# Column sums of the modulation moved into the next head pair, and an earlier low-rank load and gate tile at the start of the recurrent stage

## The reference, cut to what matters

```python
ada = (c @ w_ada[l] + b_ada[l])[:, None, :]
sh1, sc1, gt1, sh2, sc2, gt2 = jnp.split(ada, 6, axis=-1)
h = rms_norm(x, norm1_w[l]) * (1.0 + sc1) + sh1
...
w_log = -jax.nn.softplus(-(w0 + jnp.tanh(w_low) @ w2).astype(f32)) - 0.5
a = jax.nn.sigmoid((a0 + a_low @ a2).astype(f32))
kk = heads(k * k_k)
kk = kk / jnp.maximum(jnp.sqrt(jnp.sum(kk * kk, axis=-1, keepdims=True)), 1e-12)
...
g_att, g_rwkv = jnp.split(jax.nn.sigmoid(gate_in + b_gate[l]), N_BRANCHES, axis=-1)
```

## Time and profile before

| what | us |
|---|---|
| median of 3 runs | 2282.11 |
| the 3 runs | 2280.17, 2282.11, 2284.14 |
| profiled execution: span from first to last instruction | 2275.2 |
| TensorE busy in it | 2149.8 |
| GpSimd busy | 1039.4 |
| VectorE busy | 1204.5 |
| ScalarE busy | 554.5 |

### The profile page before, as it was taken

The page is one execution under the profiler, slowest core; times in us unless marked ns, Lnnn a source line. Parts: engine busy times, 40 slices in busy tenths (PEclk is TensorE's granted clock), DMA queues, the critical chain, the costliest instruction groups (busy, mean ns, idle before and its releaser), DMA issues.

```text
span 2275.2 us, 39545 instructions
## 1 busy us (share of the span) xinstructions
PE 2149.8 (94%) x16109; PEld 1712.5 (75%) x16109; DVE 1204.5 (53%) x1607; ACT 554.5 (24%) x1206; POOL 1039.4 (46%) x764
## 2 busy tenths in 40 slices
PE   8999999999989989999889999999997899999998
PEld 6888777777767777788857767777676677888886
DVE  7888525466676660301276555665553555656423
ACT  2100012333342121312322222222322213333201
POOL 7777764353443446163343321233101465666663
PEclk9999999999998989999989999999997999999999
DMA  4233222234333322031222211122002332223221
GB/s 134 93 100 104 92 86 82 88 127 143 122 128 114 102 74 93 26 104 47 78 68 59 60 41 51 30 60 59 13 23 85 113 121 80 93 92 101 97 87 66
DMA packets 180343, 189.97 MB, mean 83 GB/s; under 512 B 8142, under 2 KB 161373, under 8 KB 179933
## 3 DMA queue, kind: packets, MB, share of 16 engines
q1 hardware_dynamic: 172288, 181.81, 25.1%
q10 hardware_dynamic: 7900, 5.94, 0.9%
HBM read 179.30 MB, written 8.44 MB: 83 GB/s over the span
## 4 chain that ended last, share of the span: by engine, by line
PE 79%; DVE 14%; ACT 2%; issue 2%; DVEq 2%; DMA 1%; ACTq 0%
PE bank L760 11%; PE bank L762 11%; PE bank L761 11%; PE bank L1293 6%; PE bank L1180 5%; PE bank L1385 3%; PE bank L895 3%; PE bank L897 3%; PE bank L896 3%; PE bank L988 2%; PE bank L790 1%; PE bank L791 1%; PE bank L792 1%; DVE adaacc L2103 1%; PE bank L1196 1%
## 5 line engine op out<-in xcount | busy, mean ns | idle before, releaser
L619 POOL TENSOR_TENSOR wlo<-raws,whi 128x1024 fp32r<-128x1024 f32 (+5 forms) x316 | 684.4, 2166 | 47.3 <-issue 5.1
L617 POOL TENSOR_SCALAR whi<-raws 128x1024 fp32r<-128x1024 f32 (+5 forms) x316 | 334.6, 1059 | 647.6 <-PE bank L1180 270.3
L760 PE MATMUL bank<-hbuf,whi 128*128 128x512 f32 (+2 forms) x840 | 328.5, 391 | 0.0
L762 PE MATMUL bank<-hbuf,wlo 128*128 128x512 f32 (+2 forms) x840 | 327.5, 390 | 0.0
L761 PE MATMUL bank<-hbuf,whi 128*128 128x512 f32 (+2 forms) x776 | 302.3, 390 | 0.0
L593 POOL TENSOR_TENSOR spare<-ones 1x1 f32<-1x1 f32 x100 | 24.1, 241 | 510.6 <-PE bank L762 275.2
L762 PEld LDWEIGHTS bank<-hbuf,wlo 128*128 128x128 f32 (+2 forms) x840 | 156.8, 187 | 34.8
L760 PEld LDWEIGHTS bank<-hbuf,whi 128*128 128x128 f32 (+2 forms) x840 | 156.9, 187 | 34.3 <-POOL wlo L619 0.2
L761 PEld LDWEIGHTS bank<-hbuf,whi 128*128 128x128 f32 (+2 forms) x776 | 144.9, 187 | 31.3
L2247 DVE TENSOR_REDUCE nmax<-bank 128x4 f32<-128x512 f32 (+3 forms) x40 | 21.2, 553 | 214.5 <-PE bank L1119 149.5
L1180 PE MATMUL bank<-hbuf,whi 128*128 128x512 f32 x256 | 101.3, 446 | 0.0
(11 more groups left out here) (475 smaller groups left out, 4715.5 us busy)
## 6 DMA issues: line engine op xcount, KB each, us to landing
adaw<-in_w_ada SPq DMA_DIRECT2D x64, 384.0 KB, 4.5
raws<-in_w_up SPq DMA_DIRECT2D x22, 1024.0 KB, 5.0
raws<-in_w_in SPq DMA_DIRECT2D x41, 512.0 KB, 4.7
raws<-in_w_in SPq DMA_DIRECT2D x18, 1024.0 KB, 5.0
raws<-in_pool_w_in SPq DMA_DIRECT2D x16, 1024.0 KB, 5.4
raws<-in_mla_w_in SPq DMA_DIRECT2D x10, 1024.0 KB, 6.6
raws<-in_pool_w_out SPq DMA_DIRECT2D x8, 1024.0 KB, 5.3
raws<-in_mla_w_out SPq DMA_DIRECT2D x8, 1024.0 KB, 5.6
```

What stands on the lines that cost most here:

```text
L617: G.tensor_scalar(h_, r_, 1.0, 1.0, ALU.mult, ALU.mult)
L619: G.tensor_tensor(l_, r_, f32(h_), ALU.subtract).then_inc(raw_split, 1)
L760: M.matmul(dst, wh, acts[k][0], start=(first and k == 0), stop=False)
L762: mm = M.matmul(dst, wl, acts[k][0], start=False, stop=(last and k == n - 1))
```

## The change

It has two parts. In the latent heads, the column sums of pair i - 1 become `condition_columns(i - 1)`, issued by TensorE inside pair i between slices 6 and 7, into bank 2; ScalarE's copy (`take_condition`) moves behind the fourth exponential of pair i; VectorE's `condition(0)` moves behind `maximum(2)` and `maximum(3)`. The last pair's sums stay where they were. At the recurrent start, the first low-rank load is issued ahead of the combination's copies, gate tile j = 1 of pair 0 is computed ahead of `key_norms(0)`, and the two gate tiles of pair 0 are taken in the order 1, 0.

```diff
--- before.py
+++ after.py
@@ -76,11 +76,14 @@
     if _i == 6:
         HEAD_USES += [("o0", 0, 0), ("o1", 0, 1)]
     if _i == 7:
-        HEAD_USES += [("o0", 1, 0), ("o1", 1, 1), ("o0", 2, 2), ("o1", 2, 3)]
+        HEAD_USES += [("o0", 1, 0), ("o1", 1, 1)]
+    if _i >= 1:
+        HEAD_USES += [("ada", _i - 1, 2)]
+    if _i == 7:
+        HEAD_USES += [("o0", 2, 2), ("o1", 2, 3)]
     if _i + 1 < HEAD_PAIRS:
         HEAD_USES += [(name, _i + 1, b) for name, b in PROJ_BANKS]
-    HEAD_USES += [("ada", _i, 0)]
-HEAD_USES += [("o0", 3, 0), ("o1", 3, 1)]
+HEAD_USES += [("ada", HEAD_PAIRS - 1, 0), ("o0", 3, 0), ("o1", 3, 1)]
 FILLS = {"pool": (12,) * 4, "pool_out": (2,) * 4, "lat": (2, 1, 2, 1), "mz": (1,) * 4,
          "heads": tuple(sum(use[2] == b for use in HEAD_USES) for b in range(4)),
          "mla_out": (2,) * 4, "att": (9,) * 4, "lora": (1, 0, 1, 1), "rkv": (8, 8, 8, 0), "mix": (4,) * 4,
@@ -207,6 +210,7 @@
 MADE_ALL = [sum(2 * (len(level) > w) for level in LEVELS) for w in range(2)]
 HEAD_ROWS = (slice(0, CH), slice(CH, P))
 GATE_BANK = (0, 6)
+GATE_ORDER = ((1, 0), (0, 1))
 LEVEL_BANK = ((1, 6), (7, 3))
 
 
@@ -399,6 +403,11 @@
             return evac[b], fill(ph, b) + t // 4 + 1
 
 
+        def lora_loads(p):
+
+            return ((lw2[0:64, :], a["w2_2"][0, :, p * P:(p + 1) * P]),
+                    (lw2[64:128, :], a["a2_2"][0, :, p * P:(p + 1) * P]))
+
         def gate_rows(p):
 
             return xT[:, p % 2 * 2 * S:(p % 2 * 2 + 2) * S]
@@ -1025,7 +1034,10 @@
                 scores(1)
                 turned(0)
                 turned(1)
-                project(i, 5, 9)
+                project(i, 5, 7)
+                if i >= 1:
+                    condition_columns(i - 1)
+                project(i, 7, 9)
                 values(0)
                 values(1)
                 scores(2)
@@ -1049,6 +1061,9 @@
                 values(6)
                 values(7)
                 project(i, 29, 37)
+
+            def condition_columns(i):
+
                 pe.wait_ge(sem("ada.acc"), (i + 1) * DT)
                 cols_bank = take_bank("ada", i)
                 for t in range(6):
@@ -1060,6 +1075,7 @@
             pe.wait_ge(sem("krope"), 1)
             for i in range(HEAD_PAIRS):
                 attention(i)
+            condition_columns(HEAD_PAIRS - 1)
             for n in range(16):
                 out_slice(3, n)
             pe.wait_ge(sem("m.lo"), 16)
@@ -1172,9 +1188,10 @@
             def gate_part(p, n):
 
                 part, i = divmod(n, 3)
-                j, k = divmod(part, DT)
+                turn, k = divmod(part, DT)
+                j = GATE_ORDER[min(p, 1)][turn]
                 s, odd, dst = STRIP0["rkv"] + p * 3 + 2, p % 2, bank[GATE_BANK[j]]
-                if i == 0 and j == 0 and k in (0, first_half(DT)):
+                if i == 0 and turn == 0 and k in (0, first_half(DT)):
                     strip_ready(s, int(k > 0))
                 wh, wl = [w[odd][:, k * 256 + j * P:k * 256 + (j + 1) * P] for w in (whi, wlo)]
                 mm = M.matmul(dst[:, :], wl if i == 2 else wh, h_out[k][int(i == 1)],
@@ -1412,9 +1429,11 @@
 
             pe.wait_ge(sem("cmb.used"), 4)
             lora_products(0)
+            for n in range(3 * DT):
+                gate_part(0, n)
             key_norms(0)
             pe.wait_ge(evac[0], fill("rkv", 0) + 1)
-            for n in range(6 * DT):
+            for n in range(3 * DT, 6 * DT):
                 gate_part(0, n)
             wide_part(1)
             for p in range(PAIRS):
@@ -1569,6 +1588,11 @@
                     b = HEAD_USE[name, i][0]
                     A.copy(vN[:, n * 512:(n + 1) * 512], bank[b][:, :]).then_inc(evac[b], 1)
 
+            def take_condition(i):
+                b = HEAD_USE["ada", i][0]
+                act.wait_ge(sem("ada.col"), i + 1)
+                A.copy(ada[:, i * 6:(i + 1) * 6], bank[b][:, 0:6]).then_inc(evac[b], 1)
+
             def upper_part(t):
                 act.wait_ge(sem("m.y"), t // 2 * 4 + 4)
                 A.copy(y2H[:, t * S:(t + 1) * S], tile(zm, t)).then_inc(sem("m.hi"), 1)
@@ -1609,6 +1633,8 @@
                 exponentials(3)
                 if late:
                     upper_part(late)
+                if i >= 1:
+                    take_condition(i - 1)
                 take_both(1)
                 exponentials(4)
                 exponentials(5)
@@ -1640,9 +1666,6 @@
                         A.activation(z, z, ACT.Silu).then_inc(sem("m.silu"), 1)
                 if i < 7:
                     take_values(i + 1)
-                act.wait_ge(sem("ada.col"), i + 1)
-                A.copy(ada[:, i * 6:(i + 1) * 6], bank[HEAD_USE["ada", i][0]][:, 0:6])\
-                    .then_inc(evac[HEAD_USE["ada", i][0]], 1)
 
             act.wait_ge(sem("norm.lo"), NORM0["n_kv"]["lo"] + 2)
             score_bank, turn_bank = (bank[4], bank[5]), bank[6]
@@ -1651,6 +1674,7 @@
             take_values(0)
             for i in range(HEAD_PAIRS):
                 attention(i)
+            take_condition(HEAD_PAIRS - 1)
             upper_part(14)
             upper_part(15)
 
@@ -1727,6 +1751,8 @@
                           scratch[2].rearrange(nat, p=P, h=ATT_HEADS)).then_inc(sem("st.f0"), 16)
             act.wait_ge(sem("st.f0"), 16)
             act.wait_ge(sem("att.pv"), units_before)
+            for dst, src in lora_loads(0):
+                act.dma_start(dst, src).then_inc(sem("lw.ld"), 16)
             for pr in range(4):
                 if pr >= 1:
                     act.wait_ge(sem("cmb.pe"), pr)
@@ -1744,8 +1770,7 @@
             A.activation(glow[0:32, S:2 * S], glow[0:32, S:2 * S], ACT.Sigmoid).then_inc(sem("lora.act"), 1)
 
             def load_lora(p):
-                for dst, src in ((lw2[0:64, :], a["w2_2"][0, :, ds(p * P, P)]),
-                                 (lw2[64:128, :], a["a2_2"][0, :, ds(p * P, P)])):
+                for dst, src in lora_loads(p):
                     act.dma_start(dst, src).then_inc(sem("lw.ld"), 16)
 
             def load_gate(p):
@@ -1847,7 +1872,6 @@
                 A.activation(aT[p % 2][:, :], bank[3][:, :], ACT.Copy, scale=SCAN_SCALE ** -2).then_inc(sem("gn.y"), 1)
 
             act.wait_ge(sem("att.at"), 4)
-            load_lora(0)
             key_squares(0)
             sigmoids(0)
             load_lora(1)
@@ -2142,9 +2166,9 @@
                 if i == 6:
                     lower_part(6)
                     lower_part(7)
-                condition(0)
                 maximum(2)
                 maximum(3)
+                condition(0)
                 divide(2)
                 divide(3)
                 condition(1)
@@ -2387,13 +2411,13 @@
 
             def take_gates(q):
 
-                for j in range(2):
-                    if j == 0:
+                for turn, j in enumerate(GATE_ORDER[min(q, 1)]):
+                    if turn == 0:
                         if q < 2:
                             dve.wait_ge(sem("x_kept"), 16)
                         else:
                             dve.wait_ge(sem("gt.kept"), (q - 1) * 16)
-                    product_ready(STRIP0["rkv"] + q * 3 + 2, j)
+                    product_ready(STRIP0["rkv"] + q * 3 + 2, turn)
                     V.tensor_copy(tile(xT, q % 2 * 2 + j), bank[GATE_BANK[j]][:, :]).then_inc(sem("gt.taken"), 1)
 
             def centred(p):
```

## The result

| | median us (runs) | profiled execution: time, span |
|---|---|---|
| before | 2281.14 (6; 2278.66 to 2284.14) | span 2275.2 |
| after | 2266.36 (6; 2265.15 to 2273.91) | 2266.18, span 2264.4 |

The ratio is 0.9931, interval 0.991 to 0.9952: 14.8 us or 0.65% less, where 2266.0 was forecast. The two profiled spans differ by 10.8 us only.

What follows compares the result with a forecast made beforehand. TensorE, busy 2149.8 of 2275.2 us, was taken as the bound. Terms 6.5 + 3.2 + 6.2 + 1.5 - 1.0 = 16.4 us less gave a span of about 2258.8; with 6.9 to the median, 2266 us, range 2260 to 2273.

Steps and rivals of the forecast that it cites:

- ends of pairs 0 to 4: Latent heads: TensorE's 1.31 us wait for VectorE before the column sums goes at five pair ends, 6.5 us less.
- pair 5: End of pair 5: moving the sums saves 5.4 to 7.0 us, VectorE being late with low parts; 6.2 taken.
- pair 6: End of pair 6: VectorE late again, so 1.5 us less; 4.4 with the slow clock counted.
- clock behind pairs 0 and 1: Stretch from `scores(0)` to `scores(1)`: both clock falls gone, 2 x (6.2 - 4.6) = 3.2 us less.
- recurrent start: Start of the recurrent stage: 0.3 of the 9.9 us weight wait gained, charges against it; counted 1.0 us slower.
- The wait of `scores(1)`: Behind pair 5: a new TensorE wait of 3.9 us that may lower the clock once more, costing 1.6.
- the four waits forecast: Recurrent start: waits of about 3, 2, 4 and 4 us before low-rank products, both key sums and bonus sums.
- The charge for GpSimd: Recurrent start: GpSimd's earlier strips delay VectorE, between 0 and two or three delays of 1.4 us; 0.5 taken.
- The charge of 1.0: Whole recurrent part counted as 1.0 us slower, with 0.3 faster and 4 slower as ends.

Runs made afterwards that it cites:

- e9_twice: The changed kernel with the column sums of pairs 0 to 6 issued twice over, same result; 2281.64 us, 0.9999 of before.
- e4_warm: The kernel before with 6 extra 512-column products (30 in pair 5) filling TensorE's wait at pair ends; 2268.84 us, 0.9954 of before.
- e6_gated: The changed kernel with low parts of the output from pairs 5 and 6 shifted later, behind divisions of pairs 6 and 7; 2255.52 us, 0.9882 of before.
- f1_after: The changed kernel, both parts, timed once more on the second chip; 2265.17 us, 0.9925 of before.
- e2_rec: The kernel before with part 2 alone: early first low-rank load and new gate tile order; 2287.94 us, 1.0033 of before.
- e3_load: The kernel before with the early low-rank load alone, gate tiles kept in place; 2293.26 us, 1.0066 of before.

## Why the prediction was right

The time was forecast within 0.4 us, which is closer than the sum deserves: 16.4 us less were forecast, and the medians fell by 14.8. The steps are measured from the starts of `scores(0)`. In pairs 1 to 7 after is ahead of before by 2.6, 5.8, 8.8, 10.4, 11.9, 20.4 and 18.8 us, and at the last column sums by 16.1; 0.2 us by which it was late at the start of the heads is added back. The ends of pairs 0 to 4 with the clock are 11.9 + 0.2 less the 1.36 of the last sums that are still to come. Pair 5's term is 18.8 - 11.9 - 1.56; pair 6's is 1.56 and what is lost behind it, 18.8 - 16.1 less the 1.36 of the sums that come back:

| step | forecast us | measured us |
|---|---|---|
| ends of pairs 0 to 4 | 6.5 | 7.7 |
| clock behind pairs 0 and 1 | 3.2 | 3.1 |
| pair 5 | 6.2 | 5.3 |
| pair 6 | 1.5 | 0.2 |
| recurrent start | -1.0 | -0.2 |
| sum | 16.4 | 16.1 |

- *Ends of pairs.* A pair lost 40.84 - 39.28 = 1.56 us where the wait's row says 1.31. Two things aren't in the row. Idle time is counted from the modelled end of the last product (549.40 + 0.28), where the next one would have started 0.12 behind its start: 0.16 more. And the sums take 1.36 us from start to start behind the wait, 1.25 within the stream (551.43 to 552.68). e9_twice shows that the sums themselves moved and did not vanish, as assumed.
- *Clock.* Right in size and in cause, as far as one trace of e4_warm can show it: the falls went with the wait, and e4_warm took them away with the sums and VectorE's order left where they were.
- *Pair 5.* The wait of `scores(1)` was forecast at 3.9 and is 3.23, with 0.70 for VectorE's low part ahead of it; the clock fell once more, as feared.
- *Pair 6.* The term that was mis-sized. I counted the wait (about 2 forecast, 2.61 measured) but no slow clock behind it; in after the mean clock from 712 to 720 is 0.79. e6_gated and e4_warm price it: without the wait or without the quiet, pair 6 runs at full clock.
- *Recurrent start.* Right in that nothing is gained: the second key sums at 40.80 against 40.63. Of the four waits forecast (about 3, 2, 4, 4) the trace has 3.1, 0, 5.0 and 0.4, and f1_after, the same kernel, has 3.1, 3.0, 3.8 and 2.2. Where waits are missing in after, TensorE ran slow instead (0.68 from 1156.24 to 1166.04) and arrived just when the square was ready, at both key sums. The charge for GpSimd, of which I took 0.5, is there and varies: the square of the second keys is ready 40.3 us behind the combination in before, 40.8 in after and 43.2 in f1_after. The charge of 1.0 can't be told from nothing in the totals; the runs with part 2 on and off differ by +2.0 and -0.4.

In f1_after GpSimd's low parts of two strips (L628, 1.54 us each from 1174.38 and 1177.10) run beside VectorE's additions. In after they are done by 1176.90, and the same step behind them is short (timeline of f1_after, then of after):

```profile
1174.85 1.62 DVE L2397 SCALAR_TENSOR_TENSOR aT<-kk,lwd 128x512 f32<-128x512 f32 x1
...
1177.56 1.62 DVE L2400 TENSOR_TENSOR bT<-bT,cc 128x512 f32<-128x512 f32 x1
```

```profile
1177.54 0.69 DVE L2397 SCALAR_TENSOR_TENSOR aT<-kk,lwd 128x512 f32<-128x512 f32 x1
```

Not all of it held. The sum was made against a span of 2275.2, and 6.9 us were then added as an unchanged difference to the median. In all runs that list both, time and span differ by 1.7 to 1.8 us; the other 5 were the spread of executions: the profiled one of before was a quick one. Adding 6.9 comes to the same as taking 16.4 from the median, which is why the time fits. But the difference was not unchanged: in after the median lies 2.0 above the span, because its profiled execution was an ordinary one. So the span was 2264.4 where 2258.8 was forecast; the second profiled execution of the same kernel, f1_after, has 2259.3. Between the first two spans, 16.1 us are gained by the last column sums (765.80 to 749.67); 2.0 are given back until the combination ends, with a slow stretch at 1092 to 1100 that before lacks; and 3.4 after it, in stretches where before ran at 1.00 (window tables of after, then before, first columns as in the earlier trace rows):

```profile
1824.00:1836.00 12.00, 9.17 (x28) 6.98 (x27) 8.00 (x9) 2.56 (x4) 8.50 (x6) 0.72 0.41 130
1872.00:1892.00 20.00, 15.95 (x67) 13.19 (x66) 11.25 (x15) 7.08 (x10) 8.56 (x6) 0.74 0.33 106
```

```profile
1824.00:1836.00 12.00, 11.04 (x48) 8.62 (x47) 10.82 (x7) 0.00 (x0) 11.55 (x8) 1.00 0.26 87
1872.00:1892.00 20.00, 18.55 (x90) 15.23 (x89) 6.94 (x8) 4.08 (x6) 12.86 (x10) 1.00 0.32 105
```

The windows hold other work in the two kernels, since all of it came earlier, so they show where the clock was low, not what one operation lost. The fourteen traces end 1108 to 1117 us behind the combination, with no order by kernel. A profiled pair of single executions can't tell a change of 5 us in this kernel; the medians can.

## What to carry to other kernels

A wait is worth its whole length only if nothing behind it is late as well. The same reading, done at each place, gave 14.6 us for the sums and 0 for a single wait of 9.9. After a wait is removed, look at what VectorE was doing when the new wait ended; moving four pieces of output work to where nobody waited was worth another 7 to 11 us. And price a wait of TensorE as its length and the slow clock that may follow it: here 5.1 us of waits brought 3.4 us of slow clock with them.

## What the hardware showed unexpectedly

- A stop of 1.31 us, with one-column sums and short scores behind it, is followed by half clock in 6 of 15 pair ends of before, e2_rec and e3_load: behind pair 0 in all three, behind pairs 1, 3 and 4 in one each. With six extra 512-column products in the stop (1.47 us) none of the five pair ends of the one trace has it.
- The clock's part of a kernel's time varies between executions: before, unchanged, ran from 2275.07 to 2286.4 us in 16 runs on one chip, with mean clocks of 0.967 to 0.971.
- Work added made the kernel faster: e4_warm issues 72 more products and its median is 10.8 us below before.
